# A two-block transformer kernel whose front is put in another order: positions first, sums of squares on TensorE, the memory's norm deferred

## The chip, the cores and the metric
The kernel runs on one core of one Trainium2 chip. The metric is the device time of one execution in microseconds (us). The profile is one execution of the same program, with its own time.

## The reference
Two blocks over a sequence of 512 tokens of width 1024 in f32. What the change touches is the beginning of the first one, a sparse attention with an indexer:

```python
mem_n = rmsnorm(mem, g_mem)                       # 256 rows of memory
h = rmsnorm(x, g_mix[0])
q, c_kv, k_rope, q_idx, k_idx, w_idx, q_mem = split_cols(h @ w_in, A_SPLITS)
k_rope = apply_partial_rope(k_rope, cos32, sin32)  # angles from positions
q_idx = apply_partial_rope(q_idx, cos16, sin16)    # 16 heads of 64
k_idx = apply_partial_rope(k_idx, cos16, sin16)
dots = einsum('bqhd,bsd->bqhs', q_idx, k_idx)
score = einsum('bqhs,bqh->bqs', relu(dots), w_idx) # then the 128 best keys of each query
k, v = split(mem_n @ w_mem_kv)                     # memory attention, twice in the kernel
p = softmax((q_mem @ k.T) * 64 ** -0.5); o = p @ v
```

rmsnorm(x, g) is x * rsqrt(mean(x * x) + eps) * g. After the selection follow attention over the chosen keys, memory attention, output projection, gated feed-forward, then a banded-attention layer, and the second block.

## The kernel before
Everything lies feature-major: a tile is 128 features by 512 tokens, x is eight such tiles (xT). The weights come as one stream of 334 chunks of 128 x 1024 (eight blocks of 128 x 128) into two buffers, raw. A product in full f32 precision is made of three passes: ScalarE rounds a chunk to w_hi (`split_hi`), VectorE or GpSimd makes the rest w_lo (`split_lo`), the input has h_hi and h_lo likewise, and TensorE adds hi*hi, lo*hi and hi*lo (`product`, 24 products of 512 columns for one chunk in `project`). The results land in two banks, pj. Each engine has a program of its own, written out by hand in program order and joined by semaphores; SyncE (SP) issues the loads. There is no scheduler: an engine that waits holds everything behind it.

The norm of x is deferred. h is x times its gain only (`gained` on ScalarE for h_hi, `lowest` on VectorE for h_lo), and the factor comes later: squares on ScalarE (L913), added over the eight tiles on GpSimd (`add_squares`, L552), summed over partitions on TensorE against a column of ones (L1899), means on VectorE (L1137), power -0.5 on GpSimd (L565), spread over 128 partitions by transposes (`spread`, L1929), copied to fac_a by ScalarE. VectorE multiplies the tables of cosines and sines by it (tab_a), so that the rope applies it. The memory's norm is not deferred: squares (L694), sums (L1906), root, spread, and then memT * gain * factor on VectorE (hf, L1233), memn_hi on ScalarE, memn_lo on VectorE and GpSimd in turns (`apply`, `low`).

The tables are made on the chip from positions: angle (L1503), turns (L1504, L1505), reduction to one turn (L1507 to L1512), then the Sin table on ScalarE (L903, L904); once for width 64 (the indexer, tab64) and once for width 128 (tab128).

VectorE's order in the front: h_lo of x, positions and angles for width 64, means, tab_a, the copy of the key and widx columns with the factor, rope of the index key (kidx), angles for width 128, the memory's norm, rope of the attention key (a_k), the factor into tab128, the first index query. The index loop follows: eight tiles (two heads each) of six score products (L2175), ReLU on ScalarE (L950), weighting and addition on VectorE (L1588), while the projection for the tile after next stands between the scores; its VectorE part is a loop of three trips and two tiles written out. Then come 16 rounds of top-8 selection on VectorE (L1620, L1624), beside which TensorE projects the compressed keys (ckv) and the memory's keys and values. In memory attention the scores are added to a constant of zeros (`bias`, L1309), and `rsm` is the query's factor.

Of the kernel before, what the change touches and what calls it, by code (L numbers as in the profile page):

```python
# [15 lines left out]
P = 128  # L16
S = 512
D = 1024
DT = D // P
NB = S // P  # L20
CB = 8
# [39 lines left out]
ROPES = [("kidx", 1), ("krope", 1), ("idx", 8), ("aq", 8), ("bk", 2), ("bq", 8), ("nk_s", 2), ("nk_w", 2),  # L61
# [12 lines left out]
BEHIND = {"amix": None, "affn": "aout", "bmix": "down0", "bffn": "bout", "final1": "down1", "kv2": "cout",  # L74
# [10 lines left out]
HFBASE = {"mem": 0, "ckv": 8}  # L85
SPREADS = ("amix", "affn", "bmix", "bffn", "kv2")
# [64 lines left out]
def _attentions():  # L151
    made, score, unit, tile, done = {}, IDX_SCORES, 0, 0, 0
    pair = [(hh, b) for hh in range(2) for b in range(NB)]
    for name, tiles, units, branches, chunks, dv, dim, out0 in (
# [15 lines left out]
        ("sinks", 16), ("pos_k", 18), ("pos_v", 18)]  # L170
VC, NVEC = {}, 0
for _name, _count in VECS:
    VC[_name] = NVEC
    NVEC += _count
CONSTS = [("ident", P), ("causal", S), ("band", 2 * P), ("cmp", NB * NCMP), ("half", 2), ("inv128", 1), ("sgn128", 1),
          ("inv64", 1), ("sgn64", 1), ("rowvalid", 1)]
# [50 lines left out]
def build(nc, wstream, xin, memin, posin, vecin, cstin, tab2in, out):  # L227
# [5 lines left out]
    def put(name, cols, dt=f32, at=None):  # L233

        if at is None:
# [37 lines left out]
    tab64, ones = put("tab64", 2 * S), put("ones", P)  # L273
    cst, vec = put("cst", NCONST), put("vec", NVEC)
    v4, r4, mhalf = put("v4", 8), put("r4", 8), put("mhalf", 8)
    rsm, rsa, rsq, rck = put("rsm", 8), put("rsa", 8), put("rsq", 8), put("rck", 8)
    stats = put("stats", 8)
# [35 lines left out]
           "conv": fac_f, "kv2": put("fac_n", S, at=g1 + 16 * KB)}  # L313
# [29 lines left out]
    with ExitStack() as ctx:  # L343
# [69 lines left out]
        def _(sp):  # L413
            sp.dma_start(vec[:, :], vecin).then_inc(ld["vec"], 16)
            for m in range(0, DT, 2):
# [6 lines left out]
            sp.dma_start(posi[:, :], posin).then_inc(ld["pos"], 16)  # L422
# [26 lines left out]
        def sum_banks(name):  # L449

            return (*ps, *po) if name == "ckv" else (*ps, *pt)
# [85 lines left out]
        def _(pool):  # L537
            nc.gpsimd.memset(ones[:, :], 1.0)
            nc.gpsimd.memset(mhalf[:, :], -0.5)
            nc.gpsimd.memset(score[:, :], 0.0)  # L540
            nc.gpsimd.memset(v4[:, :], 1.0).then_inc(setup, 1)

# [19 lines left out]
            def inverse_root(name):  # L562

                pool.wait_ge(var_ready, STATS.index(name) + 1)
                nc.gpsimd.tensor_tensor(r4[:, :], v4[:, :], mhalf[:, :], ALU.pow).then_inc(rs_ready, 1)  # L565

            def low(name):

                src, n, _, _, hi, lo = NORM[name]
                for m in range(1, dict(NORMS)[name], 2):  # L570
                    s = HFBASE[name] + m
                    pool.wait_ge(hhi_ready, SBASE[NQ[name]] + m + 1)
                    here = slice(m * n, (m + 1) * n)
# [95 lines left out]
        def _(act):  # L669
# [1799 lines left out]
```

## Time and profile before
| | |
|---|---|
| median of 3 runs | 2414.76 us (2414.09 to 2414.77) |
| profiled execution, its own time | 2413.05 us |
| its span | 2411.1 us |
| TensorE busy | 2256.9 us, 94% |
| VectorE busy | 1303.6 us, 54% |
| ScalarE busy | 922.1 us, 38% |
| GpSimd busy | 263.3 us, 11% |
| mean granted TensorE clock | 0.96 |

Busy shares are averages over the whole span; the front is its first 70 us. PE is TensorE's products and PEld its weight loads, DVE is VectorE, ACT ScalarE, POOL GpSimd. An f32 product leaves two records in the trace.

### The profile page before, as it was taken

How to read it: one execution, taken by the hardware profiler on the slowest of the kernel's cores; microseconds unless marked ns; L12 is line 12 of the kernel's file. 1: busy time of each engine (PE TensorE's matmuls, PEld its weight loads, DVE VectorE, ACT ScalarE, POOL GpSimd, SP SyncE). 2: the span in 40 equal slices, each digit the busy share in tenths (PEclk: the TensorE clock that was granted, in tenths of full speed). 3: DMA queues.
4: the chain of work that ended last, by engine and by line, in shares of the span. 5: the costliest groups of instructions: out<-in, count | busy, mean ns of one | idle time of the engine just before them, and what ended most of it. 6: DMA issues, size and time to landing. Idle time of an engine off the chain costs nothing.

```text
span 2411.1 us, 34396 instructions
## 1 busy us (share of the span) xinstructions
PE 2256.9 (94%) x10826; PEld 1843.8 (76%) x10826; DVE 1303.6 (54%) x2538; ACT 922.1 (38%) x1845; POOL 263.3 (11%) x154
## 2 busy tenths in 40 slices
PE   5886999999999899999999999999999679999997
PEld 4665877888888678788888888888887567777776
DVE  6776444666644565466664445555543653455543
ACT  4333453322322266432223322222223324566551
POOL 3032220000001111110000210000002000021112
PEclk8898999999999999999999999999999889899888
DMA  3121111323233210122323323323222322000001
GB/s 121 52 79 62 61 61 53 100 92 104 88 104 105 71 44 26 62 97 95 100 92 105 105 96 97 97 97 100 98 87 96 105 70 87 1 19 9 18 10 70
DMA packets 50047, 182.88 MB, mean 76 GB/s; under 512 B 5552, under 2 KB 5680, under 8 KB 49840
## 3 DMA queue, kind: packets, MB, share of 16 engines
q1 hardware_dynamic: 49824, 181.35, 23.0%
q8 instruction: 44, 0.72, 0.1%
q0 software_dynamic: 144, 0.52, 0.1%
q14 instruction: 35, 0.29, 0.0%
HBM read 179.76 MB, written 2.10 MB: 75 GB/s over the span
## 4 chain that ended last, share of the span: by engine, by line
PE 83%; DVE 7%; issue 4%; ACT 3%; POOL 1%; DMA 1%; DVEq 0%; ACTq 0%; POOLq 0%; SPq 0%
PE pj L1863 68%; PE ps L2005 5%; PE po L2061 4%; PE pt L2021 2%; ACT w_hi L679 1%; PE ps L2175 1%; PE po L2046 1%; DMA raw<-in_wstream 1%; PE pj L1972 1%; DVE s_sb L1309 1%; DVE rtmp L1254 1%; DVE w_lo L1124 1%; PE po L2070 1%; ACT p_sb L765 1%; DVE rtmp L1251 0%
## 5 line engine op out<-in xcount | busy, mean ns | idle before, releaser
L1863 PE MATMUL pj<-h_hi,w_hi 128*128 128x512 f32 x1736 | 706.2, 407 | 23.6 <-DVE w_lo L1124 13.8
L1863 PE MATMUL pj<-h_lo,w_hi 128*128 128x512 f32 x1736 | 682.9, 393 | 0.0
L1863 PE MATMUL pj<-h_hi,w_lo 128*128 128x512 f32 x1736 | 682.8, 393 | 0.0
L679 ACT ACTIVATE w_hi<-raw 128x1024 fp32r<-128x1024 f32 x334 | 353.6, 1059 | 860.4 <-PE pj L1863 842.7
L1124 DVE TENSOR_TENSOR w_lo<-raw,w_hi 128x1024 fp32r<-128x1024 f32 x288 | 390.9, 1358 | 379.9 <-ACT w_hi L679 379.2
L1863 PEld LDWEIGHTS pj<-h_hi,w_hi 128*128 128x128 f32 x1736 | 330.8, 191 | 94.4 <-issue 16.9
L1863 PEld LDWEIGHTS pj<-h_hi,w_lo 128*128 128x128 f32 x1736 | 330.0, 190 | 70.6
L1863 PEld LDWEIGHTS pj<-h_lo,w_hi 128*128 128x128 f32 x1736 | 330.9, 191 | 65.3 <-issue 2.0
L1863 PE MATMUL pj<-G_hi,w_hi 128*128 128x512 f32 x704 | 277.5, 394 | 3.0 <-DVE G_lo L1372 3.0
L1863 PE MATMUL pj<-G_lo,w_hi 128*128 128x512 f32 x704 | 276.1, 392 | 0.0
L1863 PE MATMUL pj<-G_hi,w_lo 128*128 128x512 f32 x704 | 275.9, 392 | 0.0
L1309 DVE CUSTOM_DVE_ANT_0 s_sb<-ps,cst 128x256 f32<-128x256 f32 (+4 forms) x296 | 115.7, 391 | 181.5 <-PE ps L2005 128.6
L765 ACT ACTIVATE p_sb<-s_sb,stats 128x256 f32<-128x256 f32 (+4 forms) x288 | 139.9, 486 | 119.3 <-DVE stats L1322 117.8
L588 POOL TENSOR_TENSOR w_lo<-raw,w_hi 128x1024 fp32r<-128x1024 f32 x46 | 109.7, 2385 | 565.0 <-ACT w_hi L679 565.0
L1863 PEld LDWEIGHTS pj<-G_hi,w_hi 128*128 128x128 f32 x704 | 133.7, 190 | 34.2 <-DVE G_lo L1372 3.8
L1863 PEld LDWEIGHTS pj<-G_hi,w_lo 128*128 128x128 f32 x704 | 133.4, 190 | 28.1
L1863 PEld LDWEIGHTS pj<-G_lo,w_hi 128*128 128x128 f32 x704 | 133.5, 190 | 27.4
L2021 PE MATMUL pt<-cst,p_sb 128*128 128x128 f32 (+1 forms) x640 | 129.8, 285 | 24.8 <-ACT p_sb L765 24.1
L2021 PEld LDWEIGHTS pt<-cst,p_sb 128*128 128x128 f32 (+1 forms) x640 | 86.5, 148 | 75.4 <-ACT p_sb L765 39.0
L778 ACT ACTIVATE pT<-pt 128x384 f32<-128x384 f32 (+3 forms) x320 | 119.0, 372 | 64.7 <-PE pt L2021 61.7
L552 POOL TENSOR_TENSOR ssum<-sq 128x512 f32<-128x512 f32 x7 | 10.7, 1531 | 987.9 <-ACT sq L845 980.7
L552 POOL TENSOR_TENSOR ssum<-ssum,sq 128x512 f32<-128x512 f32 x42 | 63.3, 1506 | 291.2 <-ACT sq L845 286.7
(288 smaller groups left out, 2470.7 us busy)
## 6 DMA issues: line engine op xcount, KB each, us to landing
raw<-in_wstream SPq DMA_DIRECT2D x334, 512.0 KB, 3.4
xT<-in_x SPq DMA_DIRECT2D x4, 512.0 KB, 6.9
out_x<-xT SPq DMA_DIRECT2D x4, 512.0 KB, 2.7
memT<-in_mem SPq DMA_DIRECT2D x1, 1024.0 KB, 11.1
cst<-in_cst SPq DMA_DIRECT2D x1, 515.5 KB, 9.3
tab<-in_tab POOLq DMA_DIRECT2D x1, 512.0 KB, 4.9
posi<-in_pos SPq DMA_DIRECT2D x1, 256.0 KB, 8.8
vec<-in_vec SPq DMA_DIRECT2D x1, 179.0 KB, 2.4
```

What stands on the lines that cost most here:

```text
L552: nc.gpsimd.tensor_tensor(ssum[:, :], before, sq[:, (m % 2) * S:(m % 2 + 1) * S], ALU.add).then_inc(rest_summed, 1)
L588: nc.gpsimd.tensor_tensor(w_lo[:, here], raw[:, here], w_hi[:, here].bitcast(f32), ALU.subtract).then_inc(lo_ready, 1)
L679: nc.scalar.activation(w_hi[:, c.par * CW:(c.par + 1) * CW], raw[:, c.par * CW:(c.par + 1) * CW], ACT.Copy).then_inc(hi_ready, 1)
L765: nc.scalar.activation(p_sb[:, par * S:par * S + w], s_sb[:, par * S:par * S + w], ACT.Exp, scale=rsm[:, b:b + 1] if branch == "mem" else ...
L778: nc.scalar.activation(pT[rows, par * S:par * S + n], pt[par][rows, 0:n], ACT.Copy).then_inc(pT_ready, 1)
L1124: nc.vector.tensor_tensor(w_lo[:, here], raw[:, here], w_hi[:, here].bitcast(f32), ALU.subtract).then_inc(lo_ready, 1)
L1254: link(nc.vector.tensor_tensor(rtmp[:, :], rtmp[:, :], tab[:, S:2 * S], ALU.mult))
L1309: nc.vector.tensor_tensor_reduce(out=s_sb[:, par * S:par * S + w], in0=ps[par][:, 0:w], in1=bias(ph, u), scale=1.0, scalar=-3.0e38, op0=AL ...
L1863: mm = nc.tensor.matmul(acc, w[:, col:col + P], x[part], start=first and k == 0, stop=last and k == 2)
L2005: nc.tensor.matmul(ps[u % 2][:, 0:w], q[:, par * S + b * P:par * S + (b + 1) * P], keys, start=True, stop=True).then_inc(score_done, 1)
L2021: mm = nc.tensor.transpose(pt[par][0:wide, k * P:(k + 1) * P], p_sb[:, par * S + k * wide:par * S + (k + 1) * wide], ident)
L2061: mm = nc.tensor.matmul(acc, pT[:, par * S + k * P:par * S + (k + 1) * P], val, start=k == 0, stop=k == kbs - 1)
```

## The change
- The queue loads positions before x. The per-partition constants (inv, sgn, half, rowvalid) move from the large array cst to the small one vec, which lands first, so angles need not wait for cst.
- GpSimd clears `score` last. ScalarE makes an 8-column Sin first, which loads its table.
- The angles are cut in two, `angles` (three operations) and `reduced` (five). Those for width 64 begin before h_lo; those for width 128 stand around the means and behind kidx.
- x's squares are no longer added on GpSimd. ScalarE makes them after all of h_hi, and TensorE sums each against ones (`sums`), 8 tiles by 4 blocks.
- The memory's norm is deferred: memn_hi is memory times gain on ScalarE (before the index loop), memn_lo the same on VectorE, one tile in each of the eight index tiles (`lowest`). Its squares are summed by TensorE between the products of the second index query. Its factor, fac_mem, multiplies the memory scores in place of the addition of zeros, and rv scales the values' copies (two of 128 columns for one of 2 x 128).
- The rope of the attention key goes behind index tile 1, the factor into tab128 behind tile 2. VectorE's index loop is written out.

```diff
@@ SyncE
             sp.dma_start(vec[:, :], vecin).then_inc(ld["vec"], 16)
+            sp.dma_start(posi[:, :], posin).then_inc(ld["pos"], 16)
...
-            sp.dma_start(posi[:, :], posin).then_inc(ld["pos"], 16)
@@ ScalarE
+            act.wait_ge(setup, 1)
+            nc.scalar.activation(spare[:, :], mhalf[:, :], ACT.Sin)
             act.wait_ge(ld["vec"], 16)
             for m in range(DT):
                 act.wait_ge(x_loaded[m // 2], 16)
                 gained("amix", m // 2, m % 2)
-                if m >= 2:
-                    act.wait_ge(rest_summed, m - 1)
-                nc.scalar.activation(sq[:, (m % 2) * S:(m % 2 + 1) * S], xT[:, m * S:(m + 1) * S],
-                                     ACT.Square).then_inc(sq_ready, 1)
-                if m in (1, 5):
-                    split_hi(At(m // 4))
-            tables(0)
+                if m in (0, 5):
+                    split_hi(At(m // 5))
+            squares("amix", lambda m: (x_loaded[m // 2], 16))
             c, t = At(CH["afront"]), At(TL["afront"])
             split_hi(c + 2)
-            act.wait_ge(rest_used, 1)
             take(qn[:, 0:S], t, c)
+            tables(0)
             spread_factor("amix")
+            act.wait_ge(ld["mem"], 16)
+            for m in range(DT):
+                gained("mem", m // 2, m % 2)
             split_hi(c + 3)
-            act.wait_ge(rest_summed, DT - 1)
-            squares("mem", lambda m: (ld["mem"], 16))
-            tables(1)
-            norm_hi("mem")
+            split_hi(c + 4)
...
+            idx_query(0, 0)
...
+            squares("mem", lambda m: (ld["mem"], 16))
+            tables(1)
+            split_hi(At(CH["idx"] + 3))
+            idx_query(0, 1)
...
+                        take(vraw[:, 0:MEM], t, c, n=MEM)
+                        act.wait_ge(v_turned, number + 1)
+                        for b in range(MEM // P):
+                            at = b * 256 + (k - 2) * P
+                            nc.scalar.activation(mem_v[l][:, at:at + P], pt[number % 2][:, b * P:(b + 1) * P], ACT.Copy,
+                                                 scale=rv[:, b:b + 1])
@@ VectorE
                 if branch == "mem":
-                    return C("causal", 0, MEM)
+                    return fac_mem[:, :]
...
+                                               op0=ALU.mult if ph.units[u][2] == "mem" else ALU.add, op1=ALU.max,
...
-            means("mem")
-            angles(1)
-            apply("mem")
-            sines(1)
...
+            def rope_key():
+
+                t = At(TL["afront"] + 1)
+                sines(1)
+                link(rope(ktmp[:, 0:S], vraw[:, :], tab128, SHUF128, t))
+                for par in range(2):
+                    nc.vector.tensor_copy(a_k[96:P, par * S:(par + 1) * S], ktmp[96:P, 0:S])
...
+                lowest("mem", t, j)
+
+            idx_query(0, 0, 0)
+            idx_query(0, 0, 1)
+            split_lo(At(CH["idx"] + 3))
+            for t in range(8):
+                idx_tile(t // 2, t % 2, t < 6)
+                if t == 0:
+                    means("mem")
+                if t == 1:
+                    rope_key()
+                if t == 2:
+                    tables_by_factor(tab128, tab128, "amix")
@@ TensorE
             project(At(CH["afront"]), At(TL["afront"]), h_hi, h_lo, norm="amix")
+            sums("amix")
             pe.wait_ge(ld["cst"], 16)
-            sums("amix")
-            for some in (range(5), range(5, CB)):
+            for some in (range(4), range(4, CB)):
...
-            turn(At(TL["afront"] + 1), TN["widx"], qn[:, S:2 * S])
-            sums("mem")
-            idx_query(0, 1)
-            spread("mem")
+            turn(At(TL["afront"] + 1), TN["widx"])
+            for k in range(CB):
+                idx_query(0, 1, range(k, k + 1))
+                sums("mem", range(k, k + 1))
...
+            spread("mem")
             for k in range(2):
                 project(At(CH["ckv"] + k), At(TL["ckv"] + k), h_hi, h_lo)
```

Three places in the engines' orders (rows are instructions in program order). First VectorE at the very start, before (nsink and gg are small constants, h_lo the low part of h, w_lo that of the weights, posf the positions as floats):

```order
L1529 TENSOR_SCALAR nsink<-vec 128x16
L1530 TENSOR_TENSOR gg<-vec 128x8
L1166 SCALAR_TENSOR_TENSOR h_lo<-xT,vec,h_hi 128x512 x2
L1124 TENSOR_TENSOR w_lo<-raw,w_hi 128x1024
L1166 SCALAR_TENSOR_TENSOR h_lo<-xT,vec,h_hi 128x512 x4
L1124 TENSOR_TENSOR w_lo<-raw,w_hi 128x1024
L1166 SCALAR_TENSOR_TENSOR h_lo<-xT,vec,h_hi 128x512 x2
L1537 CAST posf<-posi 128x512
```

The same place of the changed kernel:

```order
L1529 TENSOR_TENSOR gg<-vec 128x8
L1532 CAST posf<-posi 128x512
L1500 TENSOR_SCALAR ang<-posf,vec 128x512
L1501 TENSOR_SCALAR turns<-ang 128x512
L1502 TENSOR_SCALAR turns<-turns 128x512
L1160 SCALAR_TENSOR_TENSOR h_lo<-xT,vec,h_hi 128x512
L1118 TENSOR_TENSOR w_lo<-raw,w_hi 128x1024
L1160 SCALAR_TENSOR_TENSOR h_lo<-xT,vec,h_hi 128x512 x5
```

The cast and three angle operations moved ahead of the first h_lo, and the first w_lo by one place.

Second, TensorE at the second index query, before (pt<-cst,qn are the transposes of the widx columns, sq the squares, ones the column of ones):

```order
L1948 MATMUL pt<-cst,qn 128x128 x4
L1906 MATMUL ps<-ones,sq 128x1 x16
L1863 MATMUL pj<-h_hi,w_hi 128x512
L1863 MATMUL pj<-h_lo,w_hi 128x512
L1863 MATMUL pj<-h_hi,w_lo 128x512
```

And of the changed kernel, one k of the eight in the middle of that query:

```order
L1863 MATMUL pj<-h_hi,w_hi 128x512
L1863 MATMUL pj<-h_lo,w_hi 128x512
L1863 MATMUL pj<-h_hi,w_lo 128x512
L1907 MATMUL pt<-ones,sq 128x1
L1907 MATMUL po<-ones,sq 128x1
```

The memory's 16 sum products, which stood ahead of the query in one run, now stand two by two behind each k.

Third, VectorE between index tiles 1 and 2 of the changed kernel (score is the running sum, memn_lo the memory's low part, tab_119 the width-128 tables, ktmp the roped key); before, nothing but the w_lo stood between two tiles:

```order
L1588 SCALAR_TENSOR_TENSOR score<-s_sb,widx,score 128x512
L1118 TENSOR_TENSOR w_lo<-raw,w_hi 128x1024
L1160 SCALAR_TENSOR_TENSOR memn_lo<-memT,vec,memn_hi 128x256
L1517 TENSOR_SCALAR tab_119<-tab_119,vec 128x512
L1244 TENSOR_TENSOR ktmp<-vraw,tab_119 128x512
L1245 STREAM_SHUFFLE rtmp<-vraw 128x512
L1248 TENSOR_TENSOR rtmp<-rtmp,tab_119 128x512
L1249 TENSOR_TENSOR ktmp<-ktmp,rtmp 128x512
L1567 COPY a_k<-ktmp 32x512 x2
L1588 SCALAR_TENSOR_TENSOR score<-s_sb,widx,score 128x256
```

Seven instructions of the key's rope and a memn_lo have come between the last score of one tile and the first of the next.

## Rows read from the trace of the kernel before
**Rows 1.** The page: its first line, and the chain by engine.
```profile
span 2411.1 us, 34396 instructions
PE 83%; DVE 7%; issue 4%; ACT 3%; POOL 1%; DMA 1%; DVEq 0%; ACTq 0%; POOLq 0%; SPq 0%
```
**Rows 2.** Waits, first 240 us: us in total, times, longest.
```profile
PE ps L2175 <- DVE qs L1255: 15.7, 1, 15.7
...
DVE rck L1631 <- POOL r L565: 8.7, 1, 8.7
```
**Rows 3.** Timeline of the front: start us, length us, what, idle before in brackets.
```profile
5.67 1.28 ACT L703 ACT_TABLE_LOAD   x1 [5.67 <-DMA xT<-in_x]
6.96 0.72 ACT L703 ACTIVATE h_hi<-xT,vec 128x512 fp32r<-128x512 f32 x1
...
7.83 0.75 DVE L1166 SCALAR_TENSOR_TENSOR h_lo<-xT,vec,h_hi 128x512 fp32r<-128x512 f32 x1 [4.30 <-ACT h_hi L703]
...
20.47 2.41 DVE L1166 SCALAR_TENSOR_TENSOR h_lo<-xT,vec,h_hi 128x512 fp32r<-128x512 f32 x2
...
24.33 0.48 DVE L1503 TENSOR_SCALAR ang<-posf,cst 128x512 f32<-128x512 f32 x1
...
24.57 1.35 PEld L1899 LDWEIGHTS ps<-ones,ssum 128*128 128x128 f32 x8
...
28.76 0.15 DVE L1137 TENSOR_SCALAR v<-ps 128x4 f32<-128x4 f32 x1
...
28.99 1.65 POOL L565 TENSOR_TENSOR r<-v,mhalf 128x8 f32<-128x8 f32 x1 [4.98 <-DVE v L1137]
...
30.70 0.65 PE L1929 MATMUL po<-cst,r 128*128 128x128 f32 x4 [1.12 <-POOL r L565]
...
31.00 1.22 DVE L1124 TENSOR_TENSOR w_lo<-raw,w_hi 128x1024 fp32r<-128x1024 f32 x1 [2.09 <-ACT w_hi L679]
...
31.39 0.60 ACT L709 ACTIVATE fac_a<-po 128x512 f32<-128x512 f32 x1
...
33.01 1.29 DVE L1525 TENSOR_TENSOR tab_a<-tab,fac_a 128x512 f32<-128x512 f32 x2
...
37.78 0.88 DVE L1554 TENSOR_SCALAR kidx<-ktmp,cst 128x512 f32<-128x512 f32 x2
```
**Rows 4.** Timeline from 39 us to the first index query.
```profile
39.15 5.28 PE L1906 MATMUL ps<-ones,sq 128*128 128x1 f32 x32
...
53.01 0.81 ACT L718 ACTIVATE memn_hi<-hf 128x256 fp32r<-128x256 f32 x2 [2.71 <-DVE hf L1233]
...
58.61 0.49 DVE L1518 TENSOR_SCALAR tab<-tab,cst 128x512 f32<-128x512 f32 x1 [0.83 <-POOL memn_lo L574]
...
62.75 1.29 DVE L1525 TENSOR_TENSOR tab<-tab,fac_a 128x512 f32<-128x512 f32 x2
```
**Rows 5.** Chain that ended last, first index tile: start, length, what.
```profile
68.14 1.21 PE ps L2175 x2
69.35 2.56 PE pj L1863 x6
...
75.37 1.38 PE pj L1863 x6
```
**Rows 6.** A steady index tile: busy time by engine, and VectorE's longest wait.
```profile
89.40:98.80 9.40, 9.40 (x38) 6.69 (x38) 7.20 (x13) 4.15 (x9) 0.00 (x0) 1.00 0.18 56
89.31 0.62 DVE L1588 SCALAR_TENSOR_TENSOR score<-s_sb,widx,score 128x384 f32<-128x384 f32 x1 [1.41 <-ACT s_sb L950]
```
**Rows 7.** First 12 us: length, busy PE PEld DVE ACT POOL, clock, DMA, GB/s.
```profile
0.00:12.00 12.00, 0.00 (x0) 0.01 (x1) 3.43 (x6) 6.32 (x9) 3.58 (x10) 1.00 0.84 300
```
**Rows 8.** Chain at the compressed keys' sums.
```profile
153.45 0.45 PE po L1906 x4
```
**Rows 9.** The same columns for one microsecond inside the memory's sums.
```profile
42.00:43.00 1.00, 0.99 (x7) 0.90 (x7) 0.00 (x0) 0.76 (x2) 0.00 (x0) 0.60 0.66 266
```
**Rows 10.** Projections alone (L1863), late stage: length, busy PE PEld, clock.
```profile
2180.00:2220.00 40.00, 8.56 (x27) 4.39 (x27) 1.00 0.04 13
```

More of the change, by code:

```diff
@@ L58 @@
     _t += _count
[L61 removed]
+ROPES = [("kidx", 1), ("idx", 8), ("aq", 8), ("bk", 2), ("bq", 8), ("nk_s", 2), ("nk_w", 2),
          ("nq", 8)]
@@ L697, in gained @@
             def gained(name, i, j):
-                _, _, gain, first, hi, _ = NORM[name]
+                src, n, gain, first, hi, _ = NORM[name]
                 m = i * 2 + j
@@ L1158, in lowest @@
             def lowest(name, m, j):
-                _, _, gain, first, hi, lo = NORM[name]
+                src, n, gain, first, hi, lo = NORM[name]
                 s = SBASE[NQ[name]] + m
@@ L1549, in _ @@
             c, t = At(CH["afront"]), At(TL["afront"])
-            complete(c + 1)
-            scaled("amix", qn[:, S:2 * S], t + 1)
             link(rope(ktmp[:, S:2 * S], qn[:, 0:S], tab_a, SHUF64, t))
             for hh in range(2):
-                last = nc.vector.tensor_scalar(kidx[:, hh * S:(hh + 1) * S], ktmp[:, S:2 * S], C("half", hh), None,
+                last = nc.vector.tensor_scalar(kidx[:, hh * S:(hh + 1) * S], ktmp[:, S:2 * S], V("half", hh), None,
                                                ALU.mult)
             last.then_inc(roped, 1)
+            complete(c + 1)
+            scaled("amix", vraw[:, :], t + 1)
             split_lo(At(CH["afront"] + 3))
-            means("mem")
-            angles(1)
-            apply("mem")
-            sines(1)
-            t = At(TL["afront"] + 1)
-            link(rope(ktmp[:, 0:S], qn[:, S:2 * S], tab128, SHUF128, t))
-            for par in range(2):
-                last = nc.vector.tensor_copy(a_k[96:P, par * S:(par + 1) * S], ktmp[96:P, 0:S])
-            last.then_inc(roped, 1)
-            tables_by_factor(tab128, tab128, "amix")
+            reduced()
+            split_lo(At(CH["afront"] + 4))
+            def rope_key():
[4 more added lines that the diff above has]
+                    nc.vector.tensor_copy(a_k[96:P, par * S:(par + 1) * S], ktmp[96:P, 0:S])
             def idx_query(i, j, half):
@@ L1890, in norm, with sums @@
                 spread(name)
-            def sums(name):
+            def sums(name, some=range(DT)):
                 n, k = NORM[name][1], dict(NORMS)[name]
@@ L1901, in sums @@
                     mm.then_inc(rest_used, 1)
-                for m in range(0 if name in BEHIND else k):
+                    return
+                for m in some[:k]:
                     pe.wait_ge(sq_ready, SQBASE[name] + m + 1)
@@ L1920, in spread @@
                 n, q = NORM[name][1], STATS.index(name)
-                root = r4
+                root = rv if name == "mem" else r4
                 if name == "ckv":
```

122 lines of the change are left out of this document (51 added, 71 removed).

## The prediction
> **What bounds the kernel.** I read the page first: the chain that ended last is 83% TensorE [rows 1], so time is won where TensorE waits. The waits of the first 240 us show two long ones [rows 2]: TensorE waited 15.7 us for the first roped index query (VectorE's L1255), and later VectorE waited 8.7 us for GpSimd's root of the compressed keys' norm. The front in order of time [rows 3] shows what VectorE does first: h_lo, then the angles, then, at 28.76, the means though TensorE's sums (24.57, 1.35 long) were ready at 26. In [rows 4] VectorE rebuilds the other angles and the whole memory norm, ropes the key from 58.61, multiplies the tables, and only then ropes the first index query; TensorE's first score starts at 68.14 [rows 5]. In the steady index loop TensorE is full (9.40 of 9.40) and VectorE has 7.20 of 9.40 [rows 6]. So the gain lies between 0 and 68 us, and what the change puts in the loop must fit into 2.2 us of VectorE's time a tile.
>
> **The x loads, h and the squares.** Positions now precede x on the queue: 0.26 MB more ahead of it, at the 300 GB/s of the first stretch [rows 7] 0.9 us. Before, x arrived at 5.67 and a table load of 1.28 followed [rows 3]; now the Sin table loads earlier, under the wait for vectors and x, so h_hi starts at about 6.6 instead of 6.96. Squares leave ScalarE's first loop, so its pace is 8 h_hi of 0.72 and 2 w_hi of about 1.05: done near 13.5 (the last x, by bytes, near 12). VectorE: positions land near 4.6 by bytes; the cast (at most 1.45, what lies between the last h_lo's end at 22.88 and 24.33) and three angle operations (1.4) are over by 7.4, then h_lo at 0.75 as at 7.83 without GpSimd beside it, where a pair took 2.41 beside ssum [rows 3]; GpSimd's additions are gone. 8 h_lo, overlapping to 0.65, and two w_lo of 1.22 end at 15. TensorE ends its first projection one k later, at 16.5; before, it began the sums at 24.57. So far 8 us.
>
> **The sums.** TensorE now sums the squares itself: 64 one-column records in place of 8. At 2.4 GHz four take 0.45 [rows 8], at 1.2 GHz eight take 1.35 [rows 3]. In the memory's 32 such records, begun at 39.15 [rows 4], the granted clock fell from 2.4 to 1.2 GHz near 42.2 (mean 0.60 in that microsecond) though TensorE was busy 0.99 of it [rows 9]. I take the same: 28 at 0.1125 (3.1 us) and 36 at 0.17 (6.1) end at 25.7. Before, they ended at 25.9: the 8 us are given back. The means are no longer late (the last angles and w_lo are done by then; the four small operations and GpSimd's 1.65 end at 28.2), but TensorE first runs 12 products. Six took 2.56 at half clock and 1.38 at full [rows 5], and that stretch, begun at 68.14, had the full clock again between 72 and 75; so I take nine at 0.427 and three at 0.23, 4.6, and the factor's transposes stand at 30.3 to 30.9, as before at 30.70 [rows 3]. Bounds: 64 records and 12 products all at the full clock 7.2 + 2.8 instead of 9.2 + 4.6 (3.8 less), all at half 10.9 + 5.1 (2.2 more).
>
> The Trainium skill's TensorE: Matmul & The Clock Gate, Part 1, says that a monitor of how busy TensorE has been lifts the throttle. If every busy microsecond counted, the sums would stay at the full clock and the time would be 3.8 us lower than my sum. By that rule the trace disagrees, 0.60 at 0.99 busy; the page's Part 4 says of transposes alone that they do not count like that.
>
> **From factor to first score.** fac_a at 31.0 (0.60), then VectorE goes straight to tab_a and the key's rope: from 33.01 to 38.66 before less 0.65 for scaling qn is 5.0 [rows 3], so kidx ends at 36.6. Then vraw 0.65, w_lo 1.22, the five later angle operations (all eight took 24.33 to 28.76 [rows 3], of which three simple ones 1.4, so 3.0), w_lo, the query's rope 2.8: ready at 45.8. TensorE is later: 12 products (2.75) to 33.6, the first index query 24 x 0.23 = 5.5 to 39.1, four transposes 0.45, then the second query, after each k of which stand four sum records. These need memory squares, which ScalarE begins after w_hi, the query's copy and widx (1.05 + 0.6 + 0.2 from 39.1) and delivers from 41.2 on; from there 7 x (0.69 + 0.45) + 0.45 = 8.4. First score at **49.6**, against 68.14: **18.5** gained. ScalarE's eight memory h_hi (0.81 a pair [rows 4], 3.3 in all) lie between 31.6 and 34.9 while TensorE runs those products; if this cover were gone they would cost their 3.3. What is late next is the second query.
>
> **Clock in that stretch and the first tile.** Before, the first tile came after 15.7 us of idleness, at 1.2 GHz: six products 2.56 instead of 1.38, and two score pairs 0.4 slower each: **2.0** gained if the clock now stands. For the mixed stretch the nearest row is a late stage where wide projections were only 27 records in 40 us among narrow ones; its clock stayed 1.00 [rows 10]. Here 3 x 512 columns stand in each 1.14 us. I take the full clock. At half, 8 x (1.28 + 0.68 - 1.14) = 6.6 more, and the 2.0 is not won.
>
> **The index loop.** VectorE gets one memn_lo a tile (256 columns; from 0.75 for 512, 0.4), means after tile 0 (0.2), the key's rope after tile 1, and two table products after tile 2 (1.29 [rows 4]). The rope is what ran from 58.61 to 62.75 [rows 4]: 4.1. Behind it in VectorE's queue stands the next tile's first score addition; the ScalarE copy of score n waits for addition n-2, and TensorE for the copy two back. So TensorE can run ahead only as far as VectorE's own wait in a tile, 1.41 [rows 6]: 4.1 + 0.4 - 1.4 = **3.1** lost, once. The table products and a memn_lo (1.7) fit into the 2.2 by then. In the last two tiles there is no projection to hide anything: two memn_lo, **0.8** lost. Bounds of both: 0, and 4.5 + 1.2. Copies of the loop written out on VectorE cost nothing visible, as the straight-line front shows no wait for issue.
>
> **Behind the loop.** From the loop's end to the root that VectorE waited 8.7 us for, the path is projections and the weight stream; VectorE's own new memn_lo is inside that wait. On the path: two transposes (half of the four in 0.65) 0.3, and four times one more ScalarE copy, of which one stands before that root: between 0 and 0.4, I take 0.2. **0.5** lost. The memory's factor in scores replaces an addition of zeros in the same instruction, the one in values is that extra copy: nothing more. All after 220 us stays.
>
> **Sum.** 18.5 + 2.0 - 3.1 - 0.8 - 0.5 = 16.1. The profiled execution had span 2411.1 and time 2413.05, giving 2397.0; the median of the timed runs is 1.7 above it, 2414.76, giving **2398.7**.
>
> **Rivals.** A: the clock falls in the mixed stretch (second query and sums): 16.1 - 8.6 = 7.5 gained, **2407.3**. For it: the fall at 42.2. Against: rows 10. Chance 0.17. B: the sums keep the full clock: 19.9 gained, **2394.9**. Against it the 0.60. Chance 0.08. C: the key's rope is absorbed wholly, 3.1 more: **2395.6**; it needs TensorE to run further ahead than the copies let it. Chance 0.07. D, the other side: the written-out loop makes VectorE the bound of every tile. It pays from 2.2 us a tile on (its spare time) and decides when eight tiles take more than 16.1 back, at 2.2 + 2.0 = 4.2 us a tile; at 5 the time is 2414.8 + 8 x 0.8 = **2421**. Nothing in the trace shows an addition that late; chance 0.02. E: the gain is given back behind the loop, the weight stream holding its old hour: **2414.8**; but each chunk's load waits for the chunk two before, not for a clock. Chance 0.02. The forecast itself, with its small bounds: 0.64.
>
> **Range and chances.** The forecast with the loop's and the clock's small bounds spans 2395 to 2402; to leave no more than 2 in 10 out I reach to B below and nearly all of A above: 2393.5 to 2407.5. A measurement tells 0.2%, 4.8 us, from no change: faster 0.95 (all but D, E and a little of A), same 0.03, slower 0.02.
>
> **What would show it.** The last h_lo done by 15; 64 records of sums from 16.5 lasting 9 us with the clock falling in them; the factor's transposes at 30, not earlier; first score at 49.6 at the full clock; a stall of 3 us in tile 2; the first selection round 16 us earlier than before; VectorE's wait for the root still there, near 8. Wrong if the second query takes 15 us, or if the loop's tiles each take more than 9.4.

## The result and the profile after

The changed kernel takes 2417.36 us (median of 20 runs, 2413.89 to 2422.76) against 2413.95 of the kernel before (20 runs, 2409.69 to 2415.54): a ratio of 1.0017, 95% interval 1.0010 to 1.0024. Forecast were 2398.7 us and a range of 2393.5 to 2407.5. The change makes nothing faster; by the interval it is 0.1 to 0.2% slower. The profiled execution took 2415.60 us.

Its page, first line and chain by engine, beside [rows 1]:

```profile
span 2413.8 us, 34422 instructions
PE 83%; DVE 7%; issue 4%; ACT 3%; POOL 1%; DMA 1%; DVEq 0%; ACTq 0%; POOLq 0%; SPq 0%
```

The front in order of time (start us, length us, what, and in brackets the idle time before), beside [rows 3] and [rows 5]:

```profile
9.31 0.72 ACT L694 ACTIVATE h_hi<-xT,vec 128x512 fp32r<-128x512 f32 x1 [7.00 <-DMA xT<-in_x]
...
20.55 0.50 PE L1907 MATMUL ps<-ones,sq 128*128 128x1 f32 x4
...
30.96 0.77 PE L1863 MATMUL pj<-h_hi,w_hi 128*128 128x512 f32 x1
...
35.39 0.60 PE L1930 MATMUL po<-cst,r 128*128 128x128 f32 x4
...
40.91 0.88 DVE L1552 TENSOR_SCALAR kidx<-ktmp,vec 128x512 f32<-128x512 f32 x2
...
56.34 0.68 PE L2176 MATMUL ps<-kidx,qs 128*128 128x256 f32 x2
```

x lands late, the 64 sums run from 20.55 to 30.96, the factor's transposes stand at 35.39, and the first score is at 56.34: 11.8 us before the 68.14 of [rows 5], where 18.5 were forecast. The windows of the same stretch (busy PE, PEld, DVE, ACT, POOL, then the granted clock) show the clock fall inside the sums and a little in the second query:

```profile
20.00:25.00 5.00, 5.00 (x41) 4.88 (x39) 1.53 (x3) 2.52 (x4) 0.00 (x0) 0.91 0.09 37
25.00:30.00 5.00, 5.00 (x25) 5.00 (x25) 0.61 (x1) 2.85 (x5) 0.00 (x0) 0.50 0.01 3
...
50.00:55.00 5.00, 5.00 (x28) 4.30 (x27) 0.36 (x1) 1.97 (x5) 0.00 (x0) 0.86 0.12 48
```

VectorE's timeline of the stretch behind, where the index loop ends, the root comes (8.7 in [rows 2]) and the last selection round is done:

```profile
132.08 0.42 DVE L1613 TENSOR_TENSOR score<-score,cst 128x256 f32<-128x256 f32 x1
...
167.34 0.16 DVE L1631 TENSOR_TENSOR rck<-r,rsa 128x4 f32<-128x4 f32 x1 [8.90 <-POOL r L567]
...
211.56 0.29 DVE L1639 TENSOR_SCALAR bias_a<-score 128x256 f32<-128x256 f32 x1 [0.21 <-DVE score L1624]
```

and the same view of the kernel before:

```profile
141.20 0.42 DVE L1613 TENSOR_TENSOR score<-score,cst 128x256 f32<-128x256 f32 x1
...
217.48 0.29 DVE L1639 TENSOR_SCALAR bias_a<-score 128x256 f32<-128x256 f32 x1 [0.21 <-DVE score L1624]
```

So 9.1 us are left at the loop's end, 5.9 when the selection ends, 4.6 at 390 us (w_hi of the same weight chunk at 390.16 and 394.75), and between 4.1 and 6.6 from there to 2025 us (w_hi of every sixth chunk). Then the last attention, which the diff doesn't touch, loses all of it and more. VectorE near 2155 us:

```profile
2153.41 0.15 DVE L1317 TENSOR_SCALAR stats<-stats 128x1 f32<-128x1 f32 x1
2157.54 0.19 DVE L1303 CUSTOM_DVE_ANT_0 s_sb<-ps,cst 128x32 f32<-128x32 f32 x1 [3.98 <-issue]
```

"issue" means that nothing the profile shows was waited for. The kernel before has at the same place a wait of 1.23 us, for ScalarE:

```profile
2160.60 0.19 DVE L1309 CUSTOM_DVE_ANT_0 s_sb<-ps,cst 128x32 f32<-128x32 f32 x1 [1.23 <-ACT p_sb L765]
```

So 2.75 of the 3.98 us are new. The wait stands behind 74 of the stage's 192 score units (L1303), the two that are taken ahead and three tiles of 24: just where VectorE's loop, tiles 1 and 2 a pass, jumps back for its second pass. The same 10 us stretches of TensorE, of after:

```profile
2150.00:2160.00 10.00, 8.51 (x58) 6.76 (x57) 3.26 (x19) 5.29 (x21) 2.36 (x1) 1.00 0.16 54
2160.00:2170.00 10.00, 8.98 (x32) 6.77 (x32) 2.40 (x17) 3.54 (x15) 2.53 (x2) 0.54 0.00 0
2170.00:2180.00 10.00, 10.00 (x34) 6.43 (x32) 3.32 (x14) 3.54 (x10) 0.00 (x0) 0.60 0.00 1
```

and of before:

```profile
2160.00:2170.00 10.00, 9.71 (x61) 7.77 (x60) 4.10 (x25) 5.61 (x25) 2.54 (x2) 1.00 0.11 42
2170.00:2180.00 10.00, 10.00 (x58) 7.33 (x56) 6.50 (x23) 5.08 (x16) 0.00 (x0) 1.00 0.00 0
```

TensorE still had work for most of VectorE's wait (3.49 of the 3.98 us); it runs out of it at the end and behind it:

```profile
2157.88 0.40 PE L2006 MATMUL ps<-cmp_k,qn 128*128 x2 [0.83 <-DVE stats L1303]
...
2161.60 0.69 PE L2071 MATMUL po<-cst,o_sb 128*128 128x128 f32 x2 [1.02 <-POOL o_sb L628]
```

The granted clock goes from 2.4 to 1.2 GHz at 2160.9 (0.54 is the mean of 2160 to 2170) and stays there to 2177.9; 34 matrix records stand in the last 10 us instead of 58. The DMA queues from 2153.5 to 2158, the gap and half a microsecond behind it (packets, MB, share of 16 engines):

```profile
q1 hardware_dynamic: 143, 0.52, 34.3%
q14 instruction: 2, 0.02, 1.0%
```

Of the two instruction packets the first (2155.36 to 2155.67) lies in the gap and the second (2157.77 to 2158.17) behind it. The same jump in the kernel before (2159 to 2164) has none beside its weight chunk:

```profile
q1 hardware_dynamic: 144, 0.52, 32.4%
```

### The profile page after: what moved, and what is told of

Same layout as the page of the kernel before. It is cut to its first block, busy times and chain, and to the rows that moved or that the text cites. A ratio compares the mean times of both kernels' runs of the same rounds, so it can differ in the third digit from the quotient of the medians.

```text
span 2413.8 us, 34422 instructions
## 1 busy us (share of the span) xinstructions
PE 2273.4 (94%) x10882; PEld 1855.7 (77%) x10882; DVE 1298.2 (54%) x2537; ACT 921.1 (38%) x1850; POOL 250.7 (10%) x143
## 4 chain that ended last, share of the span: by engine, by line
PE 83%; DVE 7%; issue 4%; ACT 3%; POOL 1%; DMA 1%; DVEq 0%; ACTq 0%; POOLq 0%; SPq 0%
PE pj L1863 68%; PE ps L2006 4%; PE po L2062 4%; PE pt L2022 2%; ACT w_hi L670 1%; DMA raw<-in_wstream 1%; PE po L2047 1%; PE ps L2176 1%; DVE s_sb L1303 1%; PE pj L1973 1%; DVE rtmp L1248 1%; DVE w_lo L1118 1%; PE po L2071 1%; ACT p_sb L757 1%; DVE rtmp L1245 1%
## 5 line engine op out<-in xcount | busy, mean ns | idle before, releaser
L1863 PE MATMUL pj<-h_hi,w_hi 128*128 128x512 f32 x1736 | 706.9, 407 | 21.0 <-DVE w_lo L1118 15.6
L1863 PE MATMUL pj<-h_lo,w_hi 128*128 128x512 f32 x1736 | 683.8, 394 | 0.0
L1863 PE MATMUL pj<-h_hi,w_lo 128*128 128x512 f32 x1736 | 683.6, 394 | 0.0
L1863 PEld LDWEIGHTS pj<-h_hi,w_hi 128*128 128x128 f32 x1736 | 331.1, 191 | 90.1 <-issue 17.1
L1863 PEld LDWEIGHTS pj<-h_hi,w_lo 128*128 128x128 f32 x1736 | 330.5, 190 | 71.1
L1863 PEld LDWEIGHTS pj<-h_lo,w_hi 128*128 128x128 f32 x1736 | 331.5, 191 | 64.6 <-issue 1.4
L1863 PE MATMUL pj<-G_hi,w_hi 128*128 128x512 f32 x704 | 278.1, 395 | 3.1 <-DVE G_lo L1367 3.0
L1863 PE MATMUL pj<-G_lo,w_hi 128*128 128x512 f32 x704 | 276.0, 392 | 0.0
L1863 PE MATMUL pj<-G_hi,w_lo 128*128 128x512 f32 x704 | 275.9, 392 | 0.0
L1303 DVE CUSTOM_DVE_ANT_0 s_sb<-ps,cst 128x256 f32<-128x256 f32 (+4 forms) x264 | 102.1, 387 | 174.2 <-PE ps L2006 125.1
L1863 PEld LDWEIGHTS pj<-G_hi,w_hi 128*128 128x128 f32 x704 | 133.6, 190 | 35.1 <-DVE G_lo L1367 3.8
L1863 PEld LDWEIGHTS pj<-G_hi,w_lo 128*128 128x128 f32 x704 | 133.4, 190 | 28.2
L1863 PEld LDWEIGHTS pj<-G_lo,w_hi 128*128 128x128 f32 x704 | 133.6, 190 | 27.3
L1170 DVE TENSOR_TENSOR fr<-pj,fac_f 128x512 f32<-128x512 f32 x44 | 30.4, 692 | 105.3 <-PE pj L1863 101.1
```

The costliest lines, as they stand in the source:

```text
L1170: nc.vector.tensor_tensor(dst, pj[t.par][:, 0:n], fac[name][:, 0:n], ALU.mult).then_inc(pj_free[t.par], 1)
L1303: nc.vector.tensor_tensor_reduce(out=s_sb[:, par * S:par * S + w], in0=ps[par][:, 0:w], in1=bias(ph, u), scale=1.0, scalar=-3.0e38, op0=AL ...
L1863: mm = nc.tensor.matmul(acc, w[:, col:col + P], x[part], start=first and k == 0, stop=last and k == 2)
```

## The experiments

Times are medians beside runs of the kernel before on the same chip.

**The changed kernel again** (no edit).

> The changed kernel once more, unaltered, for a second profile. In the first one the last attention (from 2030 us on) began 4.5 us earlier than before and ended 2.7 us later, with one more stretch at half the TensorE clock (2160 to 2180 us) than in the profile of the kernel before. Theory 'moment': which stretches fall is decided by the moment at which the stage begins, so the same extra stretch is seen again within 10 us, and the time is 2414 to 2419. Theory 'chance': the stretches fall at random, the extra one is elsewhere or missing, and without it the time would be near 2409. Theory 'slower code': the change itself makes the last attention slower, and its instructions take longer at the full clock too.

2415.82 us, one run. The gap is there again, and so is the half-clock stretch (from 2158.4 to 2178.8). The front is 1.8 us earlier at the first score (54.59), its second query at the full clock.

```profile
2157.17 0.19 DVE L1303 CUSTOM_DVE_ANT_0 s_sb<-ps,cst 128x32 f32<-128x32 f32 x1 [3.91 <-issue]
```

**The last attention 5 us later.**

```
+            for _ in range(22):
+                nc.tensor.matmul(pj[t_.par][:, 0:S], w_hi[...], h_hi[:, 0:S], start=True, stop=True)
             project(At(CH["gates"]), At(TL["gates"]), h_hi, h_lo, norm="q2")
```

> The changed kernel with 22 wide products (128x512, the first one of the gates projection repeated, about 0.22 us each at the full clock, 4.9 us in all) ahead of the gates' projection near 1960 us, so that the last attention begins at the hour at which it began before the change. Theory 'moment': the hour decides which stretches of that attention run at half clock, so the time rises by less than the 4.9 us added or falls: 2412 to 2417 against 2417.4. Theories 'chance' and 'slower code': the time rises by the whole 4.9 us, 2422.

2428.77 us, ratio 1.0059 (1.0046 to 1.0072). The 22 products took 7.46 and not 4.9 us (1969.19 to 1976.65), as the clock stood at half for part of them, and the time rose by 11.4, above both expectations; the gap (4.16 us) and the stretch stay at the same place of the code, though the stage began within 2 us of its old hour. "Moment" falls. This was the first theory that I held, and it was wrong.

**x first.**

```
-            sp.dma_start(posi[:, :], posin).then_inc(ld["pos"], 16)
             for m in range(0, DT, 2):
                 ...
+            sp.dma_start(posi[:, :], posin).then_inc(ld["pos"], 16)
             sp.dma_start(cst[:, :], cstin).then_inc(ld["cst"], 16)
```

> The changed kernel with the positions loaded behind x again, and their cast and first angles behind h_lo. Theory: the 2.7 us by which h_hi begins later than forecast (9.3 instead of 6.6) is the positions' 0.25 MB ahead of x on the queue, so h_hi begins at 6.7 and TensorE's first projection ends at 17.5 to 18.5 instead of 20.7; first score 53 to 54.5 instead of 56.3; time 2 to 3 us lower unless the last attention gives it back. Rival: another cause makes x late, and h_hi stays at 9.

2413.85 us (2409.88 to 2422.21), ratio 1.0006 (0.9996 to 1.0016). That is 3.5 us under the changed kernel by the medians, but the intervals of the two ratios overlap.

```profile
5.76 0.72 ACT L694 ACTIVATE h_hi<-xT,vec 128x512 fp32r<-128x512 f32 x1 [3.45 <-DMA xT<-in_x]
```

h_hi starts at 5.76 instead of 9.31 (8.14 in the second profile): 2.4 to 3.6 us for 0.26 MB. Over all profiles h_hi starts at 7.71 to 9.46 in the seven with positions first (mean 8.68) and at 5.38 to 5.95 in the five with x first (mean 5.71), 3.0 us apart. The first projection ends 2.0 us earlier (sums from 18.56), the first score stands at 52.72, and most of it is kept.

**x's squares added up by GpSimd** (as before the change).

```
+            add_squares("amix")
             inverse_root("amix")
```

> The changed kernel with the squares of x added up by GpSimd again (four one-column records of sums on TensorE instead of 64), everything else as changed. Theory: the 64 records (10.4 us, clock down to half in them, and the 12 products behind at half clock) are what keeps the factor's transposes at 35.4; GpSimd's additions slow h_lo again (2.4 us a pair instead of 1.3) so the first projection ends near 25, the sums at 26, and the transposes come at 29 to 31; first score near 51, time 4 to 5 us lower. Rival: the means come later than that, and the transposes stay near 35.

2417.15 us (2410.08 to 2420.99), ratio 1.0013 (1.0002 to 1.0024). The sums start at 27.81 and the transposes stand at 34.25, 0.9 to 1.1 us sooner than with 64 records and not 5. The clock is half there with 8 records of sums too (23.5 to 33.8, from before they start), and again from 47.4 to 61.1 in the second query, which put the first score at 59.02. The 64 records are not what costs the front its time.

**VectorE's loop written out.**

```
             trips = (ph.tiles - 1 - tail) // 2
+            if links and ph.name == "nq":
+                for j in range(1, ph.tiles - tail):
+                    tile(ph, 0, j)
+                trips = 0
```

> The changed kernel with VectorE's two passes of the loop in the last attention written out (tiles 1 to 4), the other engines as they are. In all four profiles of kernels with the changed front VectorE stands still for 3.9 to 4.2 us near 2155, where its loop of that attention jumps back; the profile names nothing that it waited for ('issue'), an instruction fetch of 8 KB ends at that moment, and behind it the TensorE clock is half for 17 to 20 us. The kernel before has neither, with the same loop 38 instructions earlier in VectorE's program. Theory 'code position': VectorE's jump back reaches code that is no longer held, because the 38 added instructions shifted the loop; without the jump the gap and the half-clock stretch go, and the time falls by 10 us to 2406 to 2408. Theory 'moment': they stay, 2417.

2403.38 us (2396.65 to 2409.40), ratio 0.9962 (0.9949 to 0.9976): 14 us under the changed kernel, more than the 10 expected. (The expectation lets an instruction fetch end at the moment at which VectorE goes on; it ended at 2155.67, 1.9 us before.) No gap, and the clock stands through the same stretches:

```profile
2160.00:2170.00 10.00, 9.98 (x70) 8.50 (x69) 7.82 (x29) 6.46 (x20) 0.00 (x0) 1.00 0.00 0
2170.00:2180.00 10.00, 10.00 (x67) 7.90 (x67) 5.66 (x22) 6.55 (x19) 3.38 (x2) 1.00 0.00 1
```

**The kernel before with 38 idle instructions at VectorE's start.**

```
+            for _ in range(38):
+                settle(dve)
             dve.wait_ge(ld["vec"], 16)
```

> The kernel before with 38 idle instructions (increments of an unused semaphore) at VectorE's start, where it waits for the first load anyway, so that its last attention's loop stands where the change puts it. Theory 'code position': the 4 us gap at the jump back appears, the half-clock stretch behind it too, and the time rises by 9 to 11 us to 2423 to 2425 with no other change. Theory 'moment' or 'slower code': nothing happens, 2413 to 2415.

2423.48 us (2421.59 to 2425.97), ratio 1.0041 (1.0027 to 1.0055): 10.1 us for instructions that do nothing. They delay VectorE's first operation from 3.29 to 5.93 us, which costs nothing there: the first score starts at 67.86 (68.14 before). The gap and the half clock appear where the kernel before has none:

```profile
2165.76 0.19 DVE L1309 CUSTOM_DVE_ANT_0 s_sb<-ps,cst 128x32 f32<-128x32 f32 x1 [4.14 <-issue]
...
2170.00:2180.00 10.00, 10.00 (x31) 7.27 (x31) 2.34 (x13) 3.30 (x12) 1.26 (x1) 0.50 0.00 0
```

**Both sums on GpSimd, ahead of the loop** (x first, written out).

```
             for k in range(CB):
-                idx_query(0, 1, range(k, k + 1))
-                sums("mem", range(k, k + 1))
+            idx_query(0, 1)
+            sums("mem")
```

> The changed kernel with x loaded ahead of the positions, the squares of x and of the memory both added up by GpSimd (4 and 2 one-column records on TensorE instead of 64 and 32), and VectorE's last attention loop written out. Theory: with x's sums by GpSimd the factor comes 1 us sooner than in the changed kernel; without sums between its products the second query takes 5.5 us at the full clock instead of 10 to 12, so the first score starts at 48 to 50 instead of 56.3; time 5 to 7 us under the changed kernel with the loop written out: 2400 to 2403. Rival: the clock falls in that stretch without the sums too, or GpSimd is late with the memory's squares; then 2405 or more.

2407.66 us, ratio 0.9979 (0.9970 to 0.9988): the rival. The first score starts at 54.86 and not at 48 to 50. ScalarE's squares wait for GpSimd's additions (0.8 to 1.6 us each), and its copy of the first query waits behind them.

**The memory's sums alone on GpSimd** (x first, written out).

> As the kernel with both sums on GpSimd, but the squares of x stay on TensorE (64 records), as the change has them; only the memory's go to GpSimd. Theory: h_lo runs without GpSimd beside it, the first projection ends 6 us sooner, but the 64 records take it back; first score 49 to 51, time within 2 us of the other: 2400 to 2404. If the 64 records are what lets the clock fall before 45 us, it is half here and not in the other.

2402.71 us, ratio 0.9957 (0.9944 to 0.9971), as expected, but the first score starts at 55.10 and not at 49 to 51. TensorE's products end at 47.36, then it stands still for 5.0 and 1.7 us; in that idleness the clock falls (half from 49.5 to 59.8). The two rows show ScalarE's late copy and the first score:

```profile
51.42 0.58 ACT L683 ACTIVATE qn<-pj 128x512 f32<-128x512 f32 x1
...
55.10 1.22 PE L2187 MATMUL ps<-kidx,qs 128*128 128x256 f32 x2 [1.71 <-DVE qs L1260]
```

**The kernel before, written out.** The control for the whole group; the edit is that of the changed kernel written out.

> The kernel before, with VectorE's loop of the last attention written out as in the run of the changed kernel (2403.4 us there). The kernel before has no gap at its jump back. Theory 'only the gap': writing out gives it nothing, 2412 to 2415, and the whole difference of about 10 us to the changed kernel written out is what the front gives. Rival 'writing out helps by itself': in the changed kernel written out a tile of that attention takes 35.6 us instead of 35.9 and the stage 5.5 us less than in the profile of before; then this kernel is at 2408 to 2410 and the front gives only 5 to 6 us.

2410.00 us (2408.87 to 2413.89), ratio 0.9987 (0.9978 to 0.9996). Writing out is worth 3.7 us by itself, so of the 10.0 between the changed kernel written out and the kernel before (0.9962) the front gives 6.3. By the intervals of the two ratios that is 6.3 with some 4 us either way.

**The key's rope in VectorE's wait for the root** (written out).

```
                 if t == 0:
                     means("mem")
-                if t == 1:
-                    rope_key()
-                if t == 2:
-                    tables_by_factor(tab128, tab128, "amix")
...
             means("ckv")
+            rope_key()
+            tables_by_factor(tab128, tab128, "amix")
```

> The changed kernel, written out, with the key's rope and its table products moved from the index loop's second and third tiles to where VectorE waits 8.9 us for GpSimd's root of the compressed keys' norm. The forecast put 3.1 us on the stall that the rope causes in the loop (TensorE's three waits there sum to 2.4). Theory: the stall goes and the wait covers the work (5.4 us): 2400 to 2401. Rival: VectorE's selection rounds behind the loop are the bound up to the next attention, so the 3 us come back as a longer wait for the root, 2403.

2404.71 us (2398.31 to 2405.11), ratio 0.9951 (0.9937 to 0.9964), which the time does not tell from 0.9962. In the profiles the loop (first copy of a score to the first addition of the causal mask) takes 71.0 us instead of 73.7, so the stall was worth some 2.7. The stretch from there to the end of the selection takes 80.6 instead of 77.9 (the mean granted clock between 132 and 165 us was 0.90 and not 0.95), and the clock had fallen in the second query (half from 47.9 to 61.5), so this single profile shows none of the gain at its end. The time lies above both expectations (2400 to 2401, and 2403 for the rival), nearer to the rival's.

**The memory's squares inside the index loop** (x first, x's sums on GpSimd, written out).

```
                 for u, (hh, b) in enumerate(IDX_UNITS):
+                    if u == 1:
+                        act.wait_ge(rest_summed, t + DT - 2)
+                        nc.scalar.activation(sq[:, j * S:j * S + MEM], memT[:, sl(t * MEM, MEM)], ACT.Square)
```

> The changed kernel, written out, x ahead of the positions, x's squares added by GpSimd, the memory's squares taken by ScalarE one in each index tile and added by GpSimd, two one-column records on TensorE behind the loop. In the kernel with both sums on GpSimd ahead of the loop ScalarE copied the second query only after the squares (51.4 us, its products had ended at 47.4), and the clock was half from 59 on. Theory: the first score comes at 47 to 48 at the full clock, 8 to 9 us before the changed kernel's, and the time is 2394 to 2398. Rival: what is won ahead of the loop is taken by VectorE's query rope (ready near 49 to 51) and by a fall of the clock behind it; then 2400 or more.

2399.58 us (2397.36 to 2404.43), ratio 0.9944 (0.9930 to 0.9958). First score at 48.45, as expected; the time is 1.6 us above its range. (Two readings in the expectation are wrong for the kernel with both sums on GpSimd: the copy at 51.4 was that of the first query, and the clock was half up to 59 and not from there, from 49.1 to 59.3.)

**Both together.**

> The squares in the loop and the key's rope in VectorE's wait together. Theory: the two add up, 3 us under the kernel with the squares in the loop alone, 2391 to 2395. Rival: same time as the better of the two, because behind the loop VectorE's rounds or the weight stream set the pace.

2397.58 us (2394.91 to 2400.67), ratio 0.9935 (0.9921 to 0.9948), the lowest median here, 19.8 us under the changed kernel. The intervals overlap with those of the squares in the loop alone, so that moving the rope adds anything is not shown; the rival may hold. First score at 47.00 and at the full clock:

```profile
47.00 0.69 PE L2190 MATMUL ps<-kidx,qs 128*128 128x256 f32 x2 [0.36 <-DVE qs L1266]
...
50.00:60.00 10.00, 10.00 (x40) 7.18 (x39) 6.87 (x11) 4.72 (x10) 1.08 (x1) 1.00 0.16 52
```

**The changed kernel's loop moved on by 218 idle instructions**, 109 in each of two places.

```
                 gated(0, 0)
+                for _ in range(109 * l):
+                    settle(dve)
                 with dve.Fori(0, FT - 1) as i:
```

> The changed kernel with 218 idle instructions in VectorE's program (109 ahead of its loop in the second feed-forward, 109 ahead of the convolution's loop, where it waits for TensorE for more than half of the time), which put its last attention's loop 256 instructions (16 KB) behind its place in the kernel before; nothing is written out. Theory 'code position, in blocks of 16 KB or a part of them': the gap of 4 us and the half-clock stretch behind it are gone, and the time is that of the kernel before less what the front gives (6.6 us by the two written-out kernels): 2406 to 2409. Rival 'any later position has the gap': 2417 or more.

2436.11 us, ratio 1.0092 (1.0078 to 1.0106). The theory of blocks of 16 KB fails: the gap is there too (4.63 us). The idle instructions themselves stopped VectorE for 9.8 and 10.0 us, and TensorE behind it (8.7 and 5.1 us), so the time says little.

```profile
1074.56 0.69 DVE L1170 TENSOR_TENSOR fr<-pj,fac_f 128x512 f32<-128x512 f32 x1 [9.76 <-issue]
...
2181.48 0.19 DVE L1303 CUSTOM_DVE_ANT_0 s_sb<-ps,cst 128x32 f32<-128x32 f32 x1 [4.63 <-issue]
```

**The kernel before with 19, and with 76.**

> The kernel before with 19 idle instructions at VectorE's start instead of 38: where the edge lies. Theory: one edge lies somewhere in the 38; gap or no gap here says in which half; the time is 2413 to 2415 without and 2421 to 2426 with the gap.

> The kernel before with 76 idle instructions at VectorE's start: behind the edge. Theory: the gap stays for every position behind the edge until the loop reaches the next block's start, so it is there at 76 too, 2421 to 2426. Rival: 38 was one bad place, and the gap is gone.

2424.59 and 2420.34 us, one run each, gaps of 4.22 and 4.23 us. The edge lies within the first 19 instructions behind the old place, and beyond it every place tried (19, 38, 76 and the far one) has the gap.

## Why the prediction was wrong

**The step that failed** is one sentence: "Copies of the loop written out on VectorE cost nothing visible, as the straight-line front shows no wait for issue", and its companion "All after 220 us stays". The copies do run without a wait where they stand. But they lengthen VectorE's program: in the two programs the last attention's loop begins 38 of VectorE's instructions later (the six written-out index tiles that replace the loop's three trips are 108 instructions for its 68; the rest of the change takes 2 away). And 2 ms later this loop, which nobody changed, jumps back and waits 3.98 us. The kernel before gets the same gap from 19 or 38 idle instructions and nothing else, and the changed kernel loses it when that loop is written out. That the place of the code decides is shown. What it costs is read twice: 10.1 us in the kernel before, and 10.3 in the changed kernel (14.0 by writing out, less the 3.7 that writing out gives without a gap). Some 3 of these are the gap, by what it exceeds the 1.2 us that the same place waits without it; the rest comes behind it, with the half clock. All nine profiles with the gap have a stretch of 17.0 to 20.5 us at 1.2 GHz that begins 0.3 to 3.4 us behind the gap, and none of the eight without it has one there; that the one brings the other rests on this count. The sum closes: 6.3 gained in front, 10.1 lost, 3.8 slower; 3.4 were measured. Without the gap the changed kernel would stand near 2407.7, just past the range's edge at 2407.5, so what the front failed to give (9.8 us) weighs as much as the gap.

That the wait is for code is inferred. In all nine profiles a packet on instruction queue q14 starts 1.4 to 2.1 us after VectorE fell idle and lasts 0.3 to 0.6 us (two packets in the kernel moved on by 218), and another starts 0.2 to 0.4 us after it went on; in the eight others q14 has no packet in the 1.2 us wait at that place. No other loop of VectorE, the longest of 147 instructions where this one has 377, shows such a wait in any profile. The Trainium skill's Runtime: NRT & Kernel Launch, Instruction fetch mechanics, says it outright: prefetch is sequential, and a taken branch whose target is not held must first fetch it by DMA; the trace agrees in that a packet comes in the wait, of 3.9 to 4.6 us in the eight kernels that have the gap. What fills the rest of the wait, ahead of the packet and the 1.9 us behind it, is not shown. A weight chunk of 0.52 MB was in flight in the same microseconds; whether the fetch waited behind it was not tried. Open is also at which places, other than that of the kernel before, the loop would fit.

Rival D had the written-out loop as the culprit, but in the wrong place: it looked for VectorE as the bound of the index tiles, and there the loop took 74.4 us instead of 71.8 (first copy of a score to the first addition of the causal mask), where the forecast's terms made it 1.9 longer: no new bound. Rival E had the right time (2414.8) by a wrong cause.

**The front, step by step**, in the profiled execution. *x loads*: 0.9 late forecast, h_hi at 6.6; it began at 9.31. Bytes over bandwidth is no price for a load put ahead of another: taking it away brought 2.4 to 3.6 us. *First projection* to 16.5: ended at 20.55, 2.7 of it x. The other 1.4 are TensorE's own pace, where the forecast let h_lo be the bound: it ran without a pause from 12.95, and its products up to 17.34 stand 0.43 us apart, the later ones 0.23. *Sums* 9.2 us with the clock falling in them: 10.4, and the fall came as described; but a record at half clock takes 0.21 us, not 0.17. The forecast read that from eight records in 1.35 us [rows 3], and of those the clock was half only up to 25.1. That they give back what the lighter h_lo wins was right: GpSimd's way is 0.9 to 1.1 us better at the transposes. *Twelve products* 4.6: 30.96 to 35.55, 4.6. *Transposes* at 30.3: 35.39. *From there to the first score* 19.3 forecast: 20.95, and 19.4 in the second profile (35.16 to 54.59), where the clock stood; the pace of 1.14 us a product triple and its sums held. *The clock in that stretch* is a matter of chance: of eight profiles in which sums stand between the second query's products it fell in four (at 47.4, 47.9, 48.0 and 49.1) and stood in four. From the transposes to the first score the four in which it stood took 19.4 each, and the others 20.95 (this profile, half for 3.4 us) and 24.8 to 24.9 (half for 13.6 us). Rival A, at 0.17, was priced too low in chance; its cost of 6.6 us was 5.4 where the clock fell for the whole stretch, and 1.6 in this profile.

*The rope's stall* 3.1: TensorE's three waits sum to 2.4 us, and taking the rope out shortened the loop by 2.7. *The loop's end*: 16.6 forecast, 9.1 found; in this profile the 6.7 missing at the first score are nearly all of the difference, and the other terms together miss by 0.8. *Behind the loop* 0.5: the term was too small. In the profiled execution 3.2 us go by the end of the selection, and 1.3 more by 390 us. 1.4 us of that are VectorE's own rounds between root and end (44.2 us instead of 42.8 here; 44.1 to 44.3 in four other profiles of changed kernels, 43.4 to 45.5 in the rest, and 42.7 to 43.3 in all five with the front of before), of which no run shows the cause; the rest goes with a longer fall of the clock in the projections ahead of the root (half from 143.6 to 150.4 here, 154.8 to 158.2 before). The root wait stayed, 8.90 for 8.7, as forecast.

A single profile does not settle the sizes, but five profiles have the changed front and loop unaltered (first score at 52.93 to 60.67), and five the front of the kernel before, three of them behind idle instructions (67.86 to 69.16). Their means are 12.7 us apart at the first score, where 18.5 were forecast, 9.5 at the loop's end (16.6), 7.3 when the selection ends and 6.5 at 490 us (16.1), which agrees with the 6.3 of the timed runs. So of 16.1 us some 6.3 were there. Mis-sized in front, in these five, are x's landing (by 1.1 to 2.9), the first projection (0.8 to 2.1), the sums with their 12 products (1.0 to 2.5) and the second query's clock (0 to 5.4); then, in the means, the index loop by 1.3 and the stretch behind it by 2.5.

## What to carry to other kernels

A change that adds instructions to an engine moves every later loop of that engine: look in the trace after for "issue" in front of the first instruction behind a jump back, in stages that the diff doesn't touch, before looking for a cause in the change. A loop of a few passes and some hundred instructions is a candidate for being written out; here that is worth 3.7 us where it fits and 14 where it doesn't. A short stall in a stage of narrow products can cost more than its length (some 3 us more of waiting became 10), so price a stall with the clock that it may take down. And work that is deferred, like a norm's factor, should have its inputs deferred as well: with both sums on GpSimd, the memory's squares ahead of the loop gave 2407.66 us and inside it 2399.58.

## What was not expected of the hardware

VectorE needs about 90 ns for an increment of a semaphore: 109 in a row took 9.8 and 10.0 us, which is not hidden even in a stage where it is half idle. 0.26 MB ahead of x on one queue delayed h_hi, which waits for x, by 3.0 us in the mean of the profiles, where its bytes at the rate of [rows 7] are 0.9 and its place in the queue's program 0.48. The granted clock's falls are not the same from one execution to the next in stages of narrow products: with the same instructions the first score stood at 56.34 and 54.59, 20.95 and 19.43 us behind the transposes. The runs show it in their spread, 8.9 us over 20 runs of the changed kernel, with mean clocks from 0.955 in the slowest to 0.958 in the fastest.
